# A seven-product second matmul in the first layer's MLP as well, with the next layer's modulation summed in pairs of columns

## What is computed

```
mod = silu(cond) @ mod_w[l] + mod_b[l]            # 6 vectors of 1024: shifts, scales, gates
h = rmsnorm(x, norm_mlp[l]) * (1 + sc2) + sh2
x = x + g2 * (square(relu(h @ mlp_w1[l])) @ mlp_w2[l])     # 1024 -> 4096 -> 1024
```

## Time and profile before

| | us |
|---|---|
| median of three runs | 2583.0 (2579.02 to 2586.45) |
| the profiled execution's own time | 2586.13 |
| its span | 2584.0 |
| PE busy | 2525.7 (98% of the span) |
| DVE busy | 1793.5 (69%) |
| ACT busy | 796.5 (31%) |
| POOL busy | 786.6 (30%) |
| one group of layer 0's MLP (617.97 / 6) | 103.0 |
| one group of layer 1's MLP (50.30 + 44.80) | 95.1 |

### The profile page before, as it was taken

How to read it: one execution, slowest core, us unless ns; L and a number is a source line. 1 busy time by engine, 2 the same in 40 slices (tenths; PEclk the granted TensorE clock), 3 DMA queues, 4 the chain that set the end, 5 groups by cost and what they waited for, 6 DMA issues and landing times.

```text
span 2584.0 us, 42040 instructions
## 1 busy us (share of the span) xinstructions
PE 2525.7 (98%) x15122; PEld 2469.2 (96%) x15122; DVE 1793.5 (69%) x3174; ACT 796.5 (31%) x1266; POOL 786.6 (30%) x575
## 2 busy tenths in 40 slices
PE   8999999999999999999999999999999999999998
PEld 6999999899999999999999888889999999999997
DVE  6888878658576585675769899956756556656674
ACT  5333323222011011021124666723422422432323
POOL 1221212322222222222223112122445445545531
PEclk8999999999999999999999999999999999999999
DMA  6422222312222222222222211132111011111131
GB/s 249 160 72 69 87 78 68 131 50 66 66 74 73 65 82 64 76 70 65 80 66 80 96 41 41 29 142 80 40 49 49 32 49 49 34 47 49 41 123 74
DMA packets 261656, 190.71 MB, mean 74 GB/s; under 512 B 9286, under 2 KB 253766, under 8 KB 260295
## 3 DMA queue, kind: packets, MB, share of 16 engines
q1 hardware_dynamic: 260004, 174.71, 22.1%
q10 hardware_dynamic: 1570, 14.93, 1.4%
HBM read 170.20 MB, written 19.41 MB: 73 GB/s over the span
## 4 chain that ended last, share of the span: by engine, by line
PE 84%; DVE 11%; issue 2%; ACT 1%; DMA 1%; SPq 0%; POOL 0%; DVEq 0%; ACTq 0%; POOLq 0%
PE psum L810 67%; PE psum L1141 12%; DVE mod_sum L1759 2%; PE psum L1191 2%; PE psum L837 1%; DVE h_lo L1792 1%; DVE h_lo L1785 1%; DVE sumsq L1730 1%; DMA mod_raw<-in_mod_w 1%; DVE x L1816 1%; DVE sumsq L1801 1%; DVE mod_sum L1754 0%; DVE s_bwd L2172 0%; DVE v_raw L2215 0%; PE psum L1006 0%
## 5 line engine op out<-in xcount | busy, mean ns | idle before, releaser
L810 PE MATMUL psum<-h_hi,w_hi 128*128 128x384 f32 (+1 forms) x2880 | 672.1, 342 | 12.3 <-POOL w_lo L700 5.2
L810 PE MATMUL psum<-h_lo,w_hi 128*128 128x384 f32 (+1 forms) x2880 | 659.0, 337 | 0.0
L810 PE MATMUL psum<-h_hi,w_lo 128*128 128x384 f32 (+1 forms) x2880 | 658.9, 337 | 0.0
L810 PEld LDWEIGHTS psum<-h_hi,w_hi 128*128 128x128 f32 x2880 | 513.3, 189 | 26.2 <-issue 13.0
L698 POOL CAST w_hi<-w_raw 128x1024 fp32r<-128x1024 f32 x120 | 127.3, 1061 | 1306.8 <-PE psum L810 794.5
L810 PEld LDWEIGHTS psum<-h_lo,w_hi 128*128 128x128 f32 x2880 | 518.0, 189 | 0.0
L810 PEld LDWEIGHTS psum<-h_hi,w_lo 128*128 128x128 f32 x2880 | 517.5, 189 | 0.0
L1759 DVE SCALAR_TENSOR_TENSOR mod_sum<-mod_raw,cond,mod_sum 128x128 f32<-128x128 f32 x1120 | 333.7, 367 | 11.1 <-DMA mod_raw<-in_mod_w 2.3
L1816 DVE SCALAR_TENSOR_TENSOR x<-psum,mod,x 128x768 f32<-128x768 f32 (+2 forms) x264 | 145.8, 610 | 236.7 <-PE psum L810 236.7
L700 POOL TENSOR_TENSOR w_lo<-w_raw,w_hi 128x1024 fp32r<-128x1024 f32 x120 | 288.4, 2403 | 9.6
L1975 DVE TENSOR_TENSOR x<-x,psum 128x576 f32<-128x576 f32 x280 | 203.6, 752 | 104.4 <-PE psum L1141 104.1
(11 more groups left out here) (300 smaller groups left out, 3083.7 us busy)
## 6 DMA issues: line engine op xcount, KB each, us to landing
w_raw<-in_mlp_w SPq DMA_DIRECT2D x128, 512.0 KB, 4.1
mod_raw<-in_mod_w SPq DMA_DIRECT2D x160, 256.0 KB, 2.9
w_raw<-in_ab_w_in SPq DMA_DIRECT2D x24, 512.0 KB, 4.5
x_spill<-x ACTq DMA_DIRECT2D x2, 4608.0 KB, 14.5
w_raw<-in_lru_w_in SPq DMA_DIRECT2D x16, 512.0 KB, 4.5
x<-x_spill SPq DMA_DIRECT2D x2, 2880.0 KB, 9.5
x_old<-x_spill SPq DMA_DIRECT2D x8, 576.0 KB, 6.8
x_rows<-in_x_sample SPq DMA_DIRECT2D x8, 512.0 KB, 6.9
```

What stands on the lines that cost most here:

```text
L810: mm = pe.matmul(psum[:, s, c, 0:end - c * CH], w, v[:, k, c * CH:end], start=(first and n == 0 and w is hi[k] and v is in_hi), stop=(last ...
```

## The change

`SPLIT_MLP` is now (0, 1): layer 0's MLP runs through `split_mlp`, and `mlp` is gone. The modulation of layer 1 is summed in pairs of columns. `pair_half(g, m)` takes a half pair, one transfer of 512 KB (four row blocks by 256 columns, `pair_raw`, one buffer), and makes 8 operations of 128 x 256 on DVE. A half of even m begins with two TENSOR_SCALAR, the rest are SCALAR_TENSOR_TENSOR. Three of the 24 pairs (six halves) go into layer 0's output projection, one half behind each of the updates 1 to 6; the other 21 go into the seven groups, six halves in each: numbers 0 to 3 between `even`/`odd` and the next `scale`, and numbers 4 and 5 two operations at a time among the reads of u = 1 and u = 2. SP loads a half only when DVE has finished the one before it, and the load stands in SP's queue between the loads of weights. The spill of x in layer 0 is split in three, and the second raw tile (`raw[1]`) is laid into the blocks' own room, `b_sum`.

```diff
-SPLIT_MLP = (1,)
+SPLIT_MLP = (0, 1)
...
+WIDE_MODS = 2
+OUT_PAIRS = GRP_PAIRS = 3
+PAIR_BUFFER = (0, 1, 0)
+PAIR_STEPS = 8
...
+            def load_half(g, m):
+
+                sp.wait_ge(pair_step, at(g, 2 * GRP_PAIRS * PAIR_STEPS, STEP0 + PAIR_STEPS * m))
+                sp.sem_inc(passed, 1)
+                w = a["mod_w"][1][m % 2 * (KT // 2 * P):(m % 2 + 1) * (KT // 2 * P)]
...
+                sp.dma_start(pair_raw[:], w.rearrange("(k p) m -> p k m", p=P)).then_inc(pair_landed, 16)
...
                     for j in range(1, GRP + 1):
                         first(g, j)
+                        if j < GRP:
+                            halves(j - 1)
                     for u in range(GRP):
                         second(g, u, U + GRP + 1 + u)
+                        if u < GRP - 1:
+                            halves(GRP - 1 + u)
...
+            def pair_columns(g, n, batch):
+
+                pe.wait_ge(pair_step, at(g, 2 * GRP_PAIRS * PAIR_STEPS, STEP0 + 2 * PAIR_STEPS * (n + 1)))
+                pe.wait_ge(mod_read, at(g, 1, FIRST_BATCHES + HEADS + batch))
...
+                        if l == 0 and j == 3 and u in (0, GRP - 1):
+                            pe.wait_ge(pair_read, at(g, PER_GROUP, READ0 + past(l, PER_GROUP) + n + 2))
+                            pair_columns(g, OUT_PAIRS + (1 if u == 0 else 2), 1)
...
+            def pair_half(g, m, first=0, end=PAIR_STEPS):
+
+                n, half = m // 2, m % 2
+                steps_done = STEP0 + PAIR_STEPS * m
+                if first == 0:
+                    dve.wait_ge(pair_landed, at(g, 32 * GRP_PAIRS, 16 * (m + 1)))
...
+                        dve.scalar_tensor_tensor(out=total, in0=w, scalar=s, in1=total, op0=ALU.mult, op1=ALU.add).then_inc(pair_step, 1)
...
+                    if l == 0 and k:
+                        pair_half(None, k - 1)
...
                         last.then_inc(pair_read, 1)
+                        if half and j in (1, 3, 5, 6):
+                            first = (1, 3, 5, 6).index(j) * 2
+                            pair_half(g, half, first, first + 2)
...
                     even(g, 0)
-                    blocks_done(g, 0)
+                    if l == 0:
+                        mods_out(1, g * GRP_MODS, GRP_MODS, at(g, GRP_MODS, MODS + GRP_MODS))
+                    halves(0)
                     scale(g, 1)
                     odd(g, 1)
+                    halves(1)
                     blocks_done(g, 6)
                     scale(g, 2)
                     even(g, 2)
+                    halves(2)
                     scale(g, 3)
                     odd(g, 3)
+                    halves(3)
                     blocks_done(g, 12)
                     scale(g, 4)
```

More of the change, by code:

```diff
@@ L254, in build, with odd_raw, raw_tile @@
         w_sum_end = blocks_at + 2 * block_bytes + 4 * 4 * 2 * P
-        raw_at = [region(TB) for _ in range(2)]
-        raw = [sb(f"raw_{n}", [TOK], raw_at[n]) for n in range(2)]
+        even_at = region(TB)
+        even_raw = sb("even_raw", [TOK], even_at)
+        pairs_at = region(2 * 4 * KT // 2 * 2 * P)
+        pair_raw = sb("pair_raw", [KT // 2, WIDE_MODS * P], pairs_at)
+        pair_sum = sb("pair_sum", [2, 2, WIDE_MODS * P], pairs_at + 4 * KT // 2 * 2 * P)
+        hid_raw = sb("hid_raw", [GRP, TOK], t_at[4])
+        def odd_raw(p):
+            return b_sum[:, p, H_O1:H_O1 + 2, :].rearrange("p b t -> p (b t)")
+        def raw_tile(j, plain=False):
+            if j % GRP == 0 or j % 2 == 0 and not plain:
+                return even_raw[:]
+            return hid_raw[:, j, :] if plain else odd_raw(j // 2)
         old_at = [blocks_at] + [t_at[8] + n * TB for n in range(5)]
@@ L554, in out_proj @@
                         sp.dma_start(x[:, 3:KT, :].rearrange("p k t -> p (k t)"), x_spill[:, 3 * TOK:]).then_inc(x_back[1], 16)
[L556 to L567, removed]
+                    if l == 0 and c > 1:
+                        load_half(None, c - 2)
             def split_mlp(l):
@@ L717, in _ @@
             split(outs, 1)
[L718 removed]
+            with pool.Fori(outs + 1, AT_MLP[0].units // 2) as i:
                 split(i, 0)
@@ L1061, in out_proj @@
                     project(None, 0, I + c, 0, U + c, width=TOK, free=out_passed if c == KT - 1 else None).then_inc(unit_done, 1)
[L1063 to L1107, removed]
@@ new lines, in out_proj @@
+                    if l == 0 and c in (4, 6):
+                        pair_columns(None, c // 2 - 2, 0)
+            def pair_columns(g, n, batch):
+                pe.wait_ge(pair_step, at(g, 2 * GRP_PAIRS * PAIR_STEPS, STEP0 + 2 * PAIR_STEPS * (n + 1)))
+                pe.wait_ge(mod_read, at(g, 1, FIRST_BATCHES + HEADS + batch))
+                start = at(g, 4 * GRP_PAIRS, 2 * (MODS + WIDE_MODS * n))
+                for e in range(WIDE_MODS):
+                    for c in range(2):
+                        column = start + 2 * e + c
+                        dst = mod_psum[:, column:column + 1] if isinstance(column, int) else mod_psum[:, ds(column, 1)]
+                        last = pe.matmul(dst, pair_sum[:, PAIR_BUFFER[n % GRP_PAIRS], c, e * P:(e + 1) * P], ones[:, 0:1], start=True, stop=True)
+                last.then_inc(mod_used, WIDE_MODS)
@@ L1413, in odd @@
                     is_squared(g, j)
-                    high(g, p, H_O1, 2, raw[1][:])
+                    high(g, p, H_O1, 2, odd_raw(p))
                     if between:
@@ L1918, in split_mlp, with scale @@
                 norm = 2 * l + 2
-                def scale(g, j):
+                def scale(g, j, plain=False):
                     s = (I + j) % 2
```

234 lines of the change are left out of this document (99 added, 135 removed).

## The result

The changed kernel takes 2637.93 us (median of four runs, 2635.44 to 2640.9) against 2583.61 before: a ratio of 1.0206, 95% interval 1.0193 to 1.0219, 54 us slower. The profiled execution has a span of 2633.6 against 2584.0.

The account below looks back on a forecast made before the run. PE, busy 98% of the span, was taken as the bound. Waits and clock of 72.8 us in seven groups, plus 7.5, 3 and 2.4, less 40.6 gained, gave +45.1: 2628 us, 1.7% slower, range 2560 to 2650.

Parts of the forecast that it names:

- the turn: PE waits for scale(4) before u = 0's third product in each layer 0 group: 5.5 us taken, 6.2 worked out.
- the seven products, moved columns and the projection's half in: Layer 0's MLP in seven-product groups gains 40.6 us; columns moved outside cost 2.4, the output projection's end 3.
- late weights for u = 3: In each group, u = 3's weights load behind half 5, so PE waits 3.7 us, bounds 0 and 5.
- clock behind the pauses: PE's clock falls to half speed behind a pause, costing 1.2 us more a group, bounds 0 and 2.4.
- unit 3 of the first group: Clearing x on DVE delays half 0 and unit 3's weights in the first group: 7.5 us once, bounds 0 and 9.
- output projection's end: Half 5 stands on DVE behind update 6, ahead of the norm: 3 us once, 2 to 5.
- What it takes away: Layer 0's MLP: groups of 95.1 + 2.4 us and a plain end of 88.2, a gain of 40.6 if nothing waits.
- The chain through SP: Within a group, loads behind halves delay units 3 and 4, pushing POOL's work over half 2; half 3 ends about 58.9.
- DVE beside POOL: DVE operations with two SBUF inputs wait for POOL's running operation: 901 ns against 345; a half alone takes 3.2 us.
- Rival 1: The halves are absorbed in layer 0's groups, losing 0 to 1.7 us a group at the turn: 2558 us, chance 0.26.

Follow-up runs that it names:

- experiment 1: Changed kernel without the 42 halves (operations and loads) in layer 0's MLP groups, modulation incomplete: 2546.55 us, ratio 0.9854 to the kernel before.
- experiment 2: Changed kernel with SP issuing each load of weights ahead of the half's load it stood behind: 2579.69 us, ratio 0.9982 to the kernel before.
- Experiment 3: Changed kernel with units 2, 3 and 4 loaded ahead of halves 0, 1 and 2, second-matmul weights still behind halves 2 to 5: 2585.75 us, ratio 1.0011.
- experiment 5: Changed kernel with each half loaded in two transfers of 256 KB, the first issued after four operations of the half before: 2618.43 us, ratio 1.0131.
- all three edits: Changed kernel with weights' loads ahead, half 3 among the reads of u = 0, and halves in transfers of 256 KB: 2561.94 us, ratio 0.9913.
- both edits: Changed kernel with all weights' loads ahead and each half in two transfers of 256 KB: 2570.33 us, ratio 0.9949 to the kernel before.

## Why the prediction was right, and where it was not

The forecast was 2628, slower, of 2560 to 2650; 2637.9 came. The mechanism is the one forecast, and experiments 1 to 3 show it for the turn, experiment 5 for u = 3; some of the terms were of another size, and their errors went both ways.

| term | forecast, us | measured, us | where it is read |
|---|---|---|---|
| the seven products, moved columns and the projection's half in | -38.2 + 3 = -35.2 | -37.5 | experiment 1 against before |
| turn, seven groups | 5.5 x 7 = 38.5 | 37.6 | waits for L1875 |
| late weights for u = 3 | 3.7 x 7 = 25.9 | 12.6 + 3.2 = 15.8 | waits in front of u = 3's first product |
| reads late in front of the columns | not listed | 3.5 | waits of L1112 |
| clock behind the pauses | 1.2 x 7 = 8.4 | about 25 | below |
| unit 3 of the first group | 7.5 | 4.5 | wait for L770 |
| output projection's end (in the first line too) | 3 | 2.6 | below |

The terms can be held against the profiled spans. The kernel without halves is 36.5 us under the one before; the waits (61.4) and the clock (25.5) on top make +50.4, and the span of the changed kernel is 49.6 longer. The medians are 54.3 apart; the profiled execution of the changed kernel is the fastest of its four.

**What it takes away: right.** 97.73 a group stands against the 97.5 worked out, and the plain end took the 88.2 of layer 1's.

**The chain through SP: right, step by step.** Half 0 done at t = 8.4 (8.8 forecast), unit 3's split at 14.2 (15.4), half 1's end at 26.5 (27.7), unit 4's split at 33.4 (34.5), half 3's end at 56.8 (58.9). I was a little pessimistic at each step, and had taken 5.5 of a worked-out 6.2 for it.

**DVE beside POOL: right, with its price now measured.** L1780 takes 732 ns in the mean in the changed kernel and 552 with the loads ahead; a half takes 3.24 to 3.25 alone (3.2 forecast) and 6.2 to 7 in the two bad places. Rival 1 had said that this would be absorbed. It was not, but it was nearly so once the loads and the transfers were changed (2561.9 with all three edits, 2558 by the rival): the rival was wrong about where POOL's work would fall, not about how much room DVE has.

```profile
L1780 DVE SCALAR_TENSOR_TENSOR pair_sum<-pair_raw,cond,pair_sum 128x256 f32<-128x256 f32 x336 | 226.0, 732 | 13.7 <-DMA pair_raw<-in_mod_w 13.7
```

**The weights of u = 3: right in kind, too large, and not alone.** I had them late by 3.7 in each group. PE waited 2.3 a group in front of u = 3's first product (15.8 / 7; 1.5 to 3.2), and each time its start follows POOL's first low part by 0.13 (experiment 5). What I had not listed is the wait beside it: DVE comes to half 5 before its transfer has landed (13.7 us idle for `pair_raw`, about two a group), and as DVE works in order, the reads behind it are late as well. The two lie on top of each other. Experiment 5 takes away the late reads and leaves 10.4 of the 15.8; experiment 2 takes away the late weights and leaves 7.9 (1.1 a group); with both edits 0.1 a group is left.

**The clock: a term a third of its size.** This is the term that was mis-sized most: 8.4 forecast, 25.5 measured. The measured clock is 17 us over its forecast, u = 3's weights are 10 under and the first group's unit 3 is 3 under, so a total within 10 us of the result owes something to luck. From the first group's unit 1 (591.42) to the plain end (1362.46) are 771.0 us; seven groups of 97.73 are 684.1; the waits listed are 61.4. That leaves 25.5, or 3.6 a group. At one pause it can be read from the chain, which gives 6.13 for the first two products behind it, where 24 matmuls of 288 columns take 3.2 (133.3 ns each), 2.9 more. Over the seven turns the chain has 4.75 to 6.13 for these 24, 1.6 to 2.9 more and 16.9 in sum; the rest stands behind the other pauses. I had scaled from nine matmuls behind one pause of 2.33 us, where other short pauses mix in, and called 1.2 the price and 2.4 the bound.

```profile
987.26 6.13 PE psum L1149 x24
```

That the clock there stays at its lower level of 1.2 GHz for longer than behind the pause in the earlier trace rows is what the rows show; why, they don't.

**The output projection's end: 2.6 of 3, by luck.** The profiled executions don't come to this place at the same time, so I count from update 6 on DVE, before (first fence) and after.

```profile
559.86 1.67 DVE L1816 SCALAR_TENSOR_TENSOR x<-psum,mod,x 128x768 f32<-128x768 f32 x3 [7.63 <-PE psum L810]
561.44 3.30 DVE L1730 TENSOR_TENSOR sumsq<-sumsq,square_out 128x1152 f32<-128x1152 f32 x1
```

```profile
556.90 1.67 DVE L1824 SCALAR_TENSOR_TENSOR x<-psum,mod,x 128x768 f32<-128x768 f32 x3 [3.75 <-PE psum L848]
559.75 6.19 DVE L1780 SCALAR_TENSOR_TENSOR pair_sum<-pair_raw,cond,pair_sum 128x256 f32<-128x256 f32 x8
567.13 1.27 DVE L1800 SCALAR_TENSOR_TENSOR h_lo<-x,gain,h_hi 128x1024 fp32r<-128x1024 f32 x1
```

From update 6 to the first L1792 it was 7.6 us (559.86 to 567.46), to the first L1800 it is 10.2 (556.90 to 567.13): 2.6 later. But half 5 takes 6.19, twice its length alone. Before, the place held an L1730 of 3.30 us and a pause of 1.29 behind ACT; my "almost without a gap" began at 566.04 and overlooked them. A half twice as long as I took it and room that I had not seen cancel.

**DVE's inputs.** Half 3 changes its length with POOL's place alone, 6.21 against 3.24 for the same eight operations (experiment 2). The Trainium skill ("GPSIMD Engine Reference", section Specifications) has VectorE and GpSimd contend for SBUF when VectorE reads two inputs there or works in a 2-port mode. The trace agrees for two inputs. The two TENSOR_SCALAR of a half, with one input tensor in SBUF, took 0.60 with POOL idle and 1.64 beside its sums (experiment 2, 935.68), so here they wait as well; whether they ran in such a mode no run shows.

**What stays open.** Of the 15 us between the best version (2561.9) and the one without halves (2546.6) some 3.4 are the six groups' 0.6; from the norm to the second group the best version takes 115.6 and the one without halves 104.0 (586.72 to 690.68), 11.7 more. That group stands behind the clearing of x (7.74 us), which I did not try to move. Experiment 3 moved the loads of units 3 and 4 together; what each is worth alone is not shown.

## What to carry to other kernels

In a queue worked in order, a load placed behind one that waits for a slow engine inherits that wait, even when its own buffer has long been free. It may still come in time for its user and cost elsewhere: here POOL's late work fell beside DVE's and doubled it. So work out not only whether a load is late, but beside what its unpacking now falls; the place of units 3 and 4 in SP's queue was worth some 50 us (2637.9 to 2585.8), nearly all of the loss of 54. And when one buffer is filled behind its last use, the engine that reads it must have something else to do for the length of the transfer, or everything behind it waits too. Where two things that an engine waits for are late by nearly the same, the view names one of them, and removing that one gains only the difference: look at the end of both (here 10.4 us of 15.8 stayed).

## What the runs showed of the hardware that I had not expected

The cost of a pause of PE is not the pause alone. The pauses of 3.9 to 6.8 us at the turn were each followed by two products that took 1.6 to 2.9 us more than at the full clock; in the fourth group the clock was 0.56 over 6.9 us. Over the seven groups the half clock took some 25 us beside 61.4 of waiting. Short pauses did not bring it everywhere: in experiment 2 one of 1.1 us in each of six groups left their clock at 1.00 (703.89 to 1303.07).

One SCALAR_TENSOR_TENSOR of 128 x 256 took 2.69 us beside a POOL operation of 2.40 in the first group (DVE at 633.46, POOL at 633.47), against 0.41 apart when POOL is idle (2.46 for six).
